# A hybrid decoder step: the sample group's paged attention rebuilt

## The chip, the cores and the metric

One core of a Trainium2 chip runs the whole step. The metric is the device time of one execution in microseconds; the kernel before has a median of 1789.56 us over 3 runs (1787.81 to 1792.38). TensorE (PE) multiplies, VectorE (DVE) and ScalarE (ACT) work element by element, GpSimd (POOL) and SyncE (SP) here mainly issue DMAs.

## The reference, cut to what matters

The step runs one decoder layer for a prompt (256 tokens) and for 8 sample sequences of 4 tokens each (32 tokens), which attend to a paged cache of 2048 past keys. Weights are shared. What the change touches is the sample group's attention:

```python
past_k = cache_k[l][page_table].reshape(8, 2048, 4, 2, 64)   # 16 pages of 128 keys for each sequence
past_v = cache_v[l][page_table].reshape(8, 2048, 4, 128)
# diff_attend, for each sequence b, head h, half c of the head:
s = einsum('bqhcd,bkhcd->bhcqk', q, k) * 64 ** -0.5          # over past and new keys, masked
p = softmax(s)                                               # over all keys
w = p[:, :, 0] - lam * p[:, :, 1]
o = einsum('bhqk,bkhe->bqhe', w, v)                          # then rms_norm over each head's 128
```

All is float32. A page of keys, and one of values, is 128 keys x 512 floats (4 heads x 128), 256 KB; there are 8 x 16 of each. Around it stand: the input projection, a state-space branch, the prompt's attention, gates, branch and output projections, a router, and a mixture of 32 experts (top 4), each with 12 MB of weights.

## The kernel before, in words

Each engine has its own program, and semaphores order them. The stages follow each other: projection (`w_in`), S5 branch and gates, the prompt's attention (to 315 us), sample attention (324 to 607 us), glu, branch, output projections and router (to about 730 us), experts (to 1750 us), and the sum of their rows. Weights and pages go through a ring of 12 slots in SBUF, each 128 partitions x 8 KB (`RING`, L124); a slot is reloaded when TensorE has freed it.

In the experts (33 jobs) each job loads 12 chunks of 1 MB by SP's queue, in a fixed order of slots (`chunk_slot`, L140), and TensorE multiplies them in float32 as two tiles of 64 columns at once, halves of the output.

Sample attention goes by sequences ("batches") i = 0 to 7. A page lies in a quarter of a slot, [128 partitions, 512 floats], loaded by `pages_of` (L421): the page number is read into a register, then one DMA of 128 rows of 2 KB. K0 to K3 (slots 0 to 3) hold the keys, V0 to V3 (4 to 7) the values, four pages each. Keys and the pages of V2 and V3 are issued by SP, V0 and V1 by GpSimd. Each slot is freed when its own pages are used.

For every page TensorE turns the four heads' keys (`keys_turn`, L1039: 4 transposes of 128x128 into one PSUM bank). ScalarE copies the bank, rounded to float32r (`key_high`, L664, recorded as L669), VectorE subtracts this from the bank (`key_low`, L1588, recorded as L1591). The query is split in the same way, high and low beside each other (64 columns), and `scores` (L1051) multiplies it with the high and the low keys, two pages at a time. ScalarE and VectorE add the two halves of the result (`scores_low`, `bank_sum`), VectorE takes the maximum over all keys, ScalarE the exps; these are turned page by page (`exps_turn`), split again, and multiplied with split values (`value_high`, `value_low`, `values`, L1078), all 16 pages into one PSUM bank. The batches are staggered: `batch(i, j)` (L1096) turns and scores batch i while it multiplies the values of batch j = i - 1. Then the sum is divided by the denominator and turned (`out_turn`), the two halves of the head are combined, and after batch 7 all is turned back, normed by head (`head_norm`, L1555) and turned again. The prompt's two tiles are normed just before the first batch.

Transposes are recorded at L893, other matmuls at L890 (a float32 matmul as two records); page DMAs at L428.

Of the kernel before, what the change touches and what calls it, by code (L numbers as in the profile page):

```python
# [32 lines left out]
NB = 8  # L33
# [29 lines left out]
E_STEP = 2  # L63
V_STEP = {3: (0, 3), 4: (3, 7), 5: (7, 10), 6: (10, 13), 7: (13, 16)}
V_BY_SP, V_BY_POOL = (2, 3), (0, 1)
# [5 lines left out]
for _name, _n in [("ident", 128), ("tri", 128), ("iota", CAP), ("ropec", 96), ("ropes", 96), ("tau", W5), ("keep", W5),  # L71
                  ("causal", 256), ("newmask", NB * NSMP), ("ones", 128), ("expert", NE), ("row", 1),
                  ("halves", P), ("jobs", NOVER)]:
    CONST_COLS[_name] = (_at, _n)
    _at += _n
# [3 lines left out]
def constants():  # L79
# [38 lines left out]
    put("halves", (i[:, None] // CAP == i[None, :] // CAP).astype(np.float32))  # L118
    put("jobs", np.broadcast_to(np.arange(NOVER), (P, NOVER)))
# [11 lines left out]
for _name, _s, _d, _r in RING:  # L131
    SLOT[_name], USE0[_name], LOAD0[_name], NDMA[_name] = _s, _uses[_s], _loads[_s], _d
    _uses[_s] += _r
    _loads[_s] += 16 * _d * _r
# [5 lines left out]
def chunk_slot(i):  # L140
    return (i + 1) % NSLOT
# [10 lines left out]
def loaded_at(name, i=0):  # L152

    return LOAD0[name] + 16 * NDMA[name] + i * (16 * NDMA[name])


def free_at(name, i=0):

    return USE0[name] + i
# [4 lines left out]
def numbered(stages):  # L164
    at, out = 0, {}
    for name, n in stages:
# [8 lines left out]
                    ("qk", 6), ("s", 8), ("oS", 1), ("oT", 3), ("bs", 8), ("ba", 8), ("out", 6), ("h2T", 5), ("lg", 3),  # L175
# [3 lines left out]
def build(nc, A):  # L179
    with ExitStack() as ctx:  # L180
# [28 lines left out]
        def at(off, *dims, n=P):  # L209
# [53 lines left out]
        keyh = rounded("keys_high", arena_at + 4 * 2304, [P, 2, H, 2 * P])  # L263
        keyl = rounded("keys_low", arena_at + 4 * (I0 + 3072), [P, 2, H, 2 * P])
        valh = rounded("values_high", arena_at + 4 * I0, [P, 3, 512])
        vall = rounded("values_low", arena_at + 4 * (I0 + 1536), [P, 3, 512])
        e2 = rounded("exps_split", arena_at + 4 * 6912, [P, NPG + 1, 2 * NSMP])
        vnh = rounded("new_values_high", arena_at + 4 * (I0 + 5120), [NSMP, 512])
        vnl = rounded("new_values_low", arena_at + 4 * (I0 + 5632), [NSMP, 512])
        oL = at(4352, 512, n=32)  # L270
        oS = at(4864, 512, n=32)
        ss = ring[0:32, 11, :]
        E = ring[0:32, 10, :]
        sm = I0 + 6144
        snw = at(sm, 32, n=32)
        En = at(sm + 32, 32, n=32)
        mx5 = at(sm + 64, 5, n=32)
        mcol = at(sm + 69, 1, n=32)
        nbias = at(sm + 70, 1, n=32)
        esum = at(sm + 71, 2, n=32)  # L280
        etot = at(sm + 73, 1, n=32)
        rden = at(sm + 74, 1, n=32)
        on = at(sm + 228, H, 2, NS)
        oTs = at(sm + 260, H, NSMP)
# [52 lines left out]
        qs = rounded("queries_split", arena_at + 4 * (K0 + 3104), [P, 72 * H + 32])  # L337
        knh = rounded("new_keys_high", arena_at + 4 * (K0 + 3424), [P, H, NSMP])
        knl = sb("new_keys_low", [P, H, NSMP], mybir.dt.float32r)
# [13 lines left out]
        s_vpool = [sem(f"values_loaded_by_gpsimd{s}") for s in V_BY_POOL]  # L353
# [18 lines left out]
        p_turned, p_keyh, p_keyl, s_group = sem("page_turned"), sem("page_high"), sem("page_low"), sem("group_scored")  # L372
        p_valh, p_vall, p_used = sem("values_page_high"), sem("values_page_low"), sem("values_page_used")
        s_qb, s_newkv, s_new, s_low, s_sum, s_nbias, s_ex, s_rden = (
            sem("q_block"), sem("new_kv_split"), sem("new_scores_done"), sem("scores_low_copied"), sem("scores_summed"),
            sem("max_ready"), sem("sample_exps"), sem("denominators"))
        s_eT, s_eh, s_el, s_pvd, s_oL, s_oS, s_oT, s_do = (
            sem("exps_turned"), sem("exps_high"), sem("exps_low"), sem("sample_pv"), sem("pv_low_copied"), sem("pv_summed"),
            sem("pv_turned"), sem("sample_out"))
# [24 lines left out]
        def wait_loaded(eng, name, i=0):  # L404
            eng.wait_ge(loaded[SLOT[name]], loaded_at(name, i))
# [15 lines left out]
        def pages_of(eng, kind, cache, b, slots=range(4)):  # L421

            for s in slots:
                name = f"{kind}{s}"
                eng.wait_ge(freed[SLOT[name]], free_at(name, b))
                for j in range(4):
                    page = eng.value_load(pages[0:1, ds(b * NPG + (4 * s + j), 1)], min_val=0, max_val=159)
                    eng.dma_start(ring[:, SLOT[name], j * 512:(j + 1) * 512],  # L428
# [96 lines left out]
        def _(act):  # L525
# [165 lines left out]
            def value_high(j, pg):  # L691
                if pg % 4 == 0:
                    wait_values(act, pg // 4, j)
# [1194 lines left out]
```

## Time and profile before

| what | us |
|---|---|
| median of 3 runs | 1789.56 |
| the profiled execution | 1789.9, its span 1788.4 |
| TensorE busy | 1457.9 |
| VectorE busy | 633.5 |
| ScalarE busy | 373.8 |

The page cuts the span into 40 equal slices of 44.7 us; a digit is the busy share in tenths. The chain of waits follows the work that ended last back from the last instruction. A group of the profile names the line, the engine, what is written and read, the shape, the number of instructions, and the mean of one.

### The profile page before, as it was taken

What the parts mean: (1) busy time and instruction counts of PE and PEld (TensorE: products, weight loads), DVE (VectorE), ACT (ScalarE), POOL (GpSimd) and SP (SyncE); (2) the same over time, 40 slices, a digit from 0 to 9 for tenths busy, and PEclk for the clock granted to TensorE, in tenths of its full rate; (3) what the DMA queues carried; (4) which work ended last, traced back from release to release, by engine and by line L of the source; (5) the groups of instructions that cost most, each with busy time, mean ns of one, the idle gap of its engine ahead of it and who ended that gap; (6) DMA issues with size and microseconds to landing.
All of it is one profiled execution on the core that took longest, in us unless ns stands there. A gap on an engine that the chain in (4) does not pass through costs nothing.

```text
span 1788.4 us, 21676 instructions
## 1 busy us (share of the span) xinstructions
PE 1457.9 (82%) x6592; PEld 669.1 (37%) x6592; DVE 633.5 (35%) x1261; ACT 373.8 (21%) x707; POOL 84.4 (5%) x151
## 2 busy tenths in 40 slices
PE   3989656688888798799998988888898989888851
PEld 2537544566666463333222222222222222222210
DVE  1367786688788522711111111111111111111104
ACT  1103223477777401100000000000000000000001
POOL 0000000011001000000000000000000000000003
PEclk7999876799899899799999999999999999999985
DMA  9220024388776822599999999999999999999974
GB/s 386 74 94 1 0 86 150 112 258 252 251 233 199 319 95 113 187 391 419 417 419 417 419 417 420 417 419 418 418 419 417 420 417 419 417 420 417 419 287 138
DMA packets 128849, 536.06 MB, mean 300 GB/s; under 512 B 20721, under 2 KB 21458, under 8 KB 92978
## 3 DMA queue, kind: packets, MB, share of 16 engines
q1 hardware_dynamic: 106914, 493.00, 69.6%
q0 software_dynamic: 10800, 34.87, 5.5%
q10 hardware_dynamic: 11104, 7.80, 1.5%
q8 instruction: 15, 0.25, 0.1%
q14 instruction: 16, 0.13, 0.0%
HBM read 519.75 MB, written 15.88 MB: 300 GB/s over the span
## 4 chain that ended last, share of the span: by engine, by line
PE 29%; DMA 24%; SPq 24%; DVE 13%; issue 6%; ACT 3%; ACTq 1%; POOL 0%; DVEq 0%; POOLq 0%
PE psum L890 24%; DMA ring<-in_w_gate_up 20%; SPq L490 12%; SPq L485 12%; PE psum L893 4%; DMA ring<-in_w_in 2%; DMA ring<-in_w_down 1%; DVE keys_low L1591 1%; DVE values_low L1595 1%; DVE ring L1602 1%; DVE ring L1477 1%; DVE arena L1854 1%; DVE ring L1478 1%; DMA arena<-in_b_down 0%; DMA ring<-expert_rows,rowi 0%
## 5 line engine op out<-in xcount | busy, mean ns | idle before, releaser
L890 PE MATMUL psum<-ring,arena 128*64 128x512 f32 (+3 forms) x3472 | 874.0, 600 | 119.3 <-DMA ring<-in_w_down 69.7
L890 PEld LDWEIGHTS psum<-ring,arena 128*64 128x64 f32 (+2 forms) x3472 | 257.8, 140 | 687.7 <-issue 412.5
L1790 DVE TENSOR_SCALAR arena<-cst,arena 128x64 f32<-128x64 f32 x105 | 20.3, 251 | 435.2 <-PE psum L890 434.9
L890 PE MATMUL psum<-arena 128*64 128x512 f32 (+5 forms) x576 | 143.6, 560 | 36.9 <-ACT ring L608 30.1
L1798 DVE COPY arena<-psum 128x512 f32<-128x512 f32 x34 | 23.5, 692 | 388.9 <-PE psum L890 386.9
L890 PE MATMUL psum<-arena,ring 128*128 128x288 f32 x480 | 129.3, 432 | 14.6 <-DMA ring<-in_w_in 8.9
L893 PE MATMUL psum<-cst,ring 128*128 128x128 f32 (+1 forms) x640 | 93.7, 298 | 35.6 <-DVE keys_low L1591 21.9
L893 PE MATMUL psum<-cst,arena 128*128 128x128 f32 (+2 forms) x455 | 72.7, 285 | 52.6 <-DVE arena L1332 15.5
L890 PEld LDWEIGHTS psum<-arena,ring 128*128 128x128 f32 x480 | 96.4, 203 | 46.1 <-DMA ring<-in_w_in 12.9
L890 PEld LDWEIGHTS psum<-arena 128*64 128x64 f32 (+2 forms) x576 | 65.6, 179 | 106.2 <-issue 61.8
L893 PEld LDWEIGHTS psum<-cst,ring 128*128 128x128 f32 (+1 forms) x640 | 77.8, 158 | 50.6 <-DVE keys_low L1591 28.4
L1591 DVE TENSOR_TENSOR keys_low<-psum,keys_high 128x512 fp32r<-128x512 f32 x128 | 82.2, 679 | 20.3 <-ACT keys_high L669 19.7
L846 POOL DMA_DIRECT2D expert_rows<-arena x66 | 34.4, 522 | 1135.2 <-ACT arena L792 1131.3
L893 PEld LDWEIGHTS psum<-cst,arena 128*128 128x128 f32 (+2 forms) x455 | 52.1, 147 | 93.2 <-issue 70.9
L1595 DVE TENSOR_TENSOR values_low<-ring,values_high 128x512 fp32r<-128x512 f32 x128 | 81.2, 680 | 9.4 <-ACT values_high L696 9.1
L696 ACT ACTIVATE values_high<-ring 128x512 fp32r<-128x512 f32 x128 | 72.4, 619 | 20.4 <-PE psum L890 20.1
L890 PE MATMUL psum<-keys_high,queries_split 128*64 128x256 f32 x256 | 74.8, 321 | 1.1 <-DVE keys_low L1591 1.1
L787 ACT ACTIVATE arena<-arena 128x512 f32<-128x512 f32 x33 | 20.8, 630 | 257.6 <-DVE arena L1802 257.6
L669 ACT ACTIVATE keys_high<-psum 128x512 fp32r<-128x512 f32 x128 | 70.7, 592 | 17.7 <-PE psum L893 16.5
L792 ACT ACTIVATE arena<-psum 128x512 f32<-128x512 f32 x33 | 19.7, 598 | 256.4 <-PE psum L890 256.4
L779 ACT ACTIVATE arena<-psum 128x512 f32<-128x512 f32 x34 | 20.3, 597 | 237.0 <-PE psum L890 237.0
L890 PE MATMUL psum<-keys_low,queries_split 128*64 128x256 f32 x256 | 68.6, 297 | 0.0
(259 smaller groups left out, 1002.6 us busy)
## 6 DMA issues: line engine op xcount, KB each, us to landing
ring<-in_w_gate_up SPq DMA_DIRECT2D x264, 1024.0 KB, 21.2
ring<-in_w_down SPq DMA_DIRECT2D x132, 1024.0 KB, 26.1
ring<-in_cache_k SPq DMA_DIRECT2D x128, 256.0 KB, 3.0
ring<-in_cache_v POOLq DMA_DIRECT2D x64, 256.0 KB, 4.3
ring<-in_cache_v SPq DMA_DIRECT2D x64, 256.0 KB, 3.0
expert_rows<-arena POOLq DMA_DIRECT2D x66, 128.0 KB, 5.8
ring<-in_w_in SPq DMA_DIRECT2D x8, 1024.0 KB, 23.7
ring<-in_w_gate SPq DMA_DIRECT2D x8, 1024.0 KB, 21.3
```

The costliest lines, as they stand in the source:

```text
L485: sp.dma_start(ring[:, s, :], wgu[ds(e, 1), k, :, :].rearrange("o p n -> p (o n)")).then_inc(loaded[s], 16)
L490: sp.dma_start(ring[:, s, :].rearrange("p (k n) -> p k n", k=2), wdn[ds(e, 1), k, :, :, :].rearrange("o p k n -> p (o k) n")).then_inc(loa ...
L669: nc.scalar.activation(keyh[:, g % 2, :, (pg % 2) * P:(pg % 2 + 1) * P], psum[:, pg % 2, :].rearrange("p (h c) -> p h c", h=H), ACT.Copy). ...
L696: nc.scalar.activation(valh[:, pg % 3, :], ring[:, SLOT[f"V{pg // 4}"], (pg % 4) * 512:(pg % 4 + 1) * 512], ACT.Copy).then_inc(p_valh, 1)
L779: nc.scalar.activation(xg, psum[:, 6, :], ACT.Copy).then_inc(e_xg, 1)
L787: nc.scalar.activation(sig, gg, ACT.Sigmoid, scale=ALPHA).then_inc(e_sig, 1)
L846: pool.dma_start(ydram[ds(j * CAP, CAP), 512 * half:512 * half + 512], y[64 * half:64 * half + 64, :]).then_inc(e_out, 16)
L890: return nc.tensor.matmul(out, lhsT=a, rhs=b, start=start, stop=stop, skip_group_check=True)
L893: return nc.tensor.transpose(out, in_, ident[0:n, 0:n])
L1591: TT(keyl[place], psum[:, pg % 2, :].rearrange("p (h c) -> p h c", h=H), keyh[place], ALU.subtract).then_inc(p_keyl, 1)
L1595: TT(vall[:, pg % 3, :], ring[:, SLOT[f"V{pg // 4}"], (pg % 4) * 512:(pg % 4 + 1) * 512], valh[:, pg % 3, :], ALU.subtract).then_inc(p_val ...
L1798: CP(xT[:, :, :], psum[:, 7, :].rearrange("p (c q) -> p c q", c=4)).then_inc(e_xs, 1)
```

## The change

Keys and values are no longer split; everything is multiplied in float32. The 16 pages of a batch are four groups of four. A page goes to 32 partitions, four rows of keys (8 KB) on each, and the four pages of a group fill the 128 partitions of one slot (`four_pages`). Group g's scores are written to partitions 32g to 32g+31 of one bank, each group on a tile of 32 columns of TensorE, and so are its values' products: each group has its own maximum, sum and output. After all batches one merge weighs the groups (`coef`) and turns the heads in the same matmuls. SP issues all keys, GpSimd all values; the values of batch b are loaded when those of b - 1 are multiplied. Branch weights go to slots 0 to 3, `w_out` to 4 to 7 after the last values, and the experts' chunks start at another slot. The sample's head norm is done by a matmul with ones; the prompt's head norms move into the first batches; the glu matmuls stand before the last values.

```diff
-RING += [(f"K{s}", s, 4, NB) for s in range(4)] + [(f"V{s}", 4 + s, 0 if s in V_BY_POOL else 4, NB) for s in range(4)]
-RING += [("w_glu", 8, 1, 1), ("w_bs0", 9, 1, 1), ("w_bs1", 10, 1, 1), ("w_ba0", 11, 1, 1), ("w_ba1", 0, 1, 1)]
-RING += [(f"w_out{k}", 1 + k, 1, 1) for k in range(4)]
+RING += [(f"K{s}", s, 4 * NB, 0) for s in range(4)]
+RING += [("w_glu", 8, 1, 1), ("w_bs0", 0, 1, 1), ("w_bs1", 1, 1, 1), ("w_ba0", 2, 1, 1), ("w_ba1", 3, 1, 1)]
+RING += [(f"w_out{k}", 4 + k, 1, 1) for k in range(4)] + [("exps", 9, 0, 1), ("pv0", 10, 0, 1), ("pv1", 11, 0, 1)]
 def chunk_slot(i):
-    return (i + 1) % NSLOT
+    return (i + 5) % NSLOT
...
+        def four_pages(eng, cache, b, g, s, done):
+            for j in range(4):
+                page = eng.value_load(pages[0:1, b * NPG + 4 * g + j:b * NPG + 4 * g + j + 1], min_val=0, max_val=159)
+                eng.dma_start(ring[32 * j:32 * j + 32, s, :],
+                              cache[ds(page, 1), :, :].rearrange("o (p q) n -> p (o q n)", q=4)).then_inc(done, 16)
...
+            def keys(b, g):                                  # SP
+                if b == 0:
+                    sp.wait_ge(freed[g], USE0[f"K{g}"])
+                else:
+                    sp.wait_ge(s_ktv, 8 * (b - 1) + 2 * g + 2)
+                four_pages(sp, ck, b, g, g, loaded[g])
...
+            sp.wait_ge(s_pvd, NB)                            # before the loads of w_out
...
+            for b in range(NB):                              # GpSimd
+                if b:
+                    pool.wait_ge(s_pvd, b)
+                for g in range(4):
+                    four_pages(pool, cv, b, g, 4 + g, s_vpool[g])
...
+            def turned_keys(i, g):                           # ScalarE: h = 0, 2; VectorE: h = 1, 3
+                for h in (0, 2):
+                    n = 16 * i + 4 * g + h
+                    act.wait_ge(s_turned, n + 1)
+                    if i:
+                        act.wait_ge(s_scored, i)
+                    nc.scalar.activation(KT[g][:, h, :], psum[:, TBANK[n % 4], :], ACT.Copy).then_inc(s_kta, 1)
...
+            def turn_keys(i, g):                             # TensorE from here on
+                pe.wait_ge(loaded[g], keys_at(g, i))
+                for h in range(H):
+                    n = 16 * i + 4 * g + h
+                    if n >= 4:
+                        pe.wait_ge((s_kta, s_ktv)[n % 2], (n - 4) // 2 + 1)
+                    for j in range(4):
+                        last = tr(psum[:, TBANK[n % 4], j * P:(j + 1) * P], ring[:, g, j * 512 + h * P:j * 512 + (h + 1) * P])
+                    last.then_inc(s_turned, 1)
+            def scores(i):
+                pe.wait_ge(s_kta, 8 * i + 8)
+                pe.wait_ge(s_ktv, 8 * i + 8)
...
+                for h in range(H):
+                    for g in range(4):
+                        last = mm(psum[32 * g:32 * g + 32, 3, :], qp[:, h, i, :], KT[g][:, h, :], h == 0, h == H - 1)
+                last.then_inc(s_scored, 1)
...
+            def values(i):
+                pe.wait_ge(s_pT, i + 1)
+                if i:
+                    pe.wait_ge(s_pvs, i)
+                for g in range(4):
+                    pe.wait_ge(s_vpool[g], 64 * (i + 1))
+                mm(psum[0:32, 5, :], pT[0:NSMP, 512:544], vt[0:NSMP, 2, :], True, False)
+                for j in range(4):
+                    for g in range(4):
+                        last = mm(psum[32 * g:32 * g + 32, 5, :], pT[:, j * P + 32 * g:j * P + 32 * g + 32],
+                                  ring[:, 4 + g, j * 512:(j + 1) * 512], j == 0 and g > 0, j == 3)
+                last.then_inc(s_pvd, 1)
...
+            for i in range(NB):
+                turn_keys(i, 0)
+                if i == 0:
+                    new_scores()
+                turn_keys(i, 1)
+                if i:
+                    exps_turn(i - 1)
+                turn_keys(i, 2)
+                turn_keys(i, 3)
+                if i:
+                    values(i - 1)
+                scores(i)
...
+            for i in range(3):
+                glu(i)
+            exps_turn(NB - 1)
...
+            glu(3)
+            values(NB - 1)
...
+            for b in range(NB):
+                for h in range(H):
+                    last = mm(psum[:, 6, h * NSMP + b * NS:h * NSMP + (b + 1) * NS], PV[:, b, h * P:(h + 1) * P],
+                              coef[:, b, h * NS:(h + 1) * NS], True, True)
+            last.then_inc(s_o, 1)
+            pe.wait_ge(s_osq, 1)
+            mm(psum[:, 6, P:2 * P], ones, o_sq, True, True).then_inc(s_osum, 1)
...
+            step(nc.vector.memset(qp, 0.0))                  # VectorE, ahead of the first batch
+            for h in range(H):
+                for c in range(2):
+                    ins = CP(qp[:, h, :, h * QC + c * NS:h * QC + (c + 1) * NS], qsmp[:, h, c])
...
+                if 1 <= i < 3:
+                    head_norm(i - 1, 128)
+                if i < 2:
+                    head_squares(i, 128)
```

## Rows read from the trace of the kernel before

**Rows 1.** The page's 40 slices: DMA share in tenths, GB/s.

```profile
DMA  9220024388776822599999999999999999999974
GB/s 386 74 94 1 0 86 150 112 258 252 251 233 199 319 95 113 187 391 419 417 419 417 419 417 420 417 419 418 418 419 417 420 417 419 417 420 417 419 287 138
```

**Rows 2.** Stretches: length, busy us (count) by engine, PEclk, DMA share, GB/s.

```profile
402.00:436.20 34.20, 28.70 (x192) 22.92 (x193) 28.32 (x56) 24.59 (x45) 4.37 (x8) 0.90 0.78 243
900.00:1300.00 400.00, 352.61 (x1553) 107.71 (x1551) 53.94 (x130) 31.52 (x52) 13.55 (x26) 1.00 1.02 418
```

**Rows 3.** The chain in order of time: start us, us, what.

```profile
419.44 1.97 PE psum L893 x8
453.61 1.97 PE psum L893 x8
```

**Rows 4.** Timeline around the stage: start us, us, engine, line, instruction [idle before <-releaser].

```profile
314.24 0.69 DVE L1550 COPY arena<-psum 128x512 f32<-128x512 f32 x1 [3.43 <-PE psum L890]
324.11 1.94 PE L893 MATMUL psum<-cst,ring 128*128 128x128 f32 x8 [9.91 <-DVEq L1669]
606.53 0.39 PE L890 MATMUL psum<-new_values_low,exps_split 32*64 32x512 f32 x1
610.75 10.44 PE L890 MATMUL psum<-arena,ring 128*128 128x288 f32 x32
624.66 3.78 PE L890 MATMUL psum<-arena,ring 128*128 128x288 f32 x10 [2.24 <-DVE arena L1690]
```

**Rows 5.** Timeline and groups of TensorE: transposes, paired tiles, 32-column matmuls, their weight loads.

```profile
405.70 1.03 PE L893 MATMUL psum<-cst,ring 128*128 128x128 f32 x8
1003.82 1.94 PE L890 MATMUL psum<-ring,arena 128*64 128x512 f32 x8 [0.54 <-DMA ring<-in_w_gate_up]
...
L890 PE MATMUL psum<-ring,arena 128*32 128x512 f32 x80 | 34.7, 593 | 0.1
L890 PEld LDWEIGHTS psum<-ring,arena 128*32 128x32 f32 x80 | 8.6, 110 | 25.3 <-issue 25.0 <-DVE arena L1357 0.3
```

**Rows 6.** Issue of pages, then of expert rows, then DMA issues (KB, us to landing).

```profile
402.62 0.55 POOL L428 DMA_DIRECT2D ring<-in_cache_v  x1 [0.67 <-issue]
403.84 0.55 POOL L428 DMA_DIRECT2D ring<-in_cache_v  x1 [0.67 <-issue]
412.55 8.47 SPq L428 DMA_DIRECT2D ring<-in_cache_v  x8
...
L846 POOL DMA_DIRECT2D expert_rows<-arena x66 | 34.4, 522 | 1135.2 <-ACT arena L792 1131.3
...
ring<-in_cache_v POOLq DMA_DIRECT2D x64, 256.0 KB, 4.3
ring<-in_cache_v SPq DMA_DIRECT2D x64, 256.0 KB, 3.0
```

**Rows 7.** Timeline: value matmuls behind idle, and warm ones.

```profile
594.06 0.69 PE L890 MATMUL psum<-values_high,exps_split 128*64 128x512 f32 x1 [1.56 <-DVE exps_split L1624]
598.45 0.54 PE L890 MATMUL psum<-values_high,exps_split 128*64 128x512 f32 x1
...
404.32 0.40 PE L890 MATMUL psum<-values_high,exps_split 128*64 128x512 f32 x1
404.55 0.39 PE L890 MATMUL psum<-values_low,exps_split 128*64 128x512 f32 x1
```

**Rows 8.** Stretches with narrow transfers (first two) and a wide one (last).

```profile
718.00:720.00 2.00, 2.00 (x12) 2.00 (x11) 1.13 (x6) 0.00 (x0) 0.00 (x0) 0.50 1.03 218
1751.00:1752.00 1.00, 0.00 (x0) 0.00 (x0) 0.00 (x0) 0.00 (x0) 0.00 (x0) 1.00 0.69 160
1784.00:1786.00 2.00, 0.00 (x0) 0.00 (x0) 1.67 (x3) 0.00 (x0) 0.00 (x0) 0.50 0.83 336
```

**Rows 9.** A memset, and the group of the router's matmuls.

```profile
276.61 1.98 DVE L1510 MEMSET arena<- 128x2304 f32 x1 [0.76 <-PE psum L893]
L890 PE MATMUL psum<-arena 128*128 128x32 f32 x32 | 7.0, 401 | 0.6 <-issue 0.6
```

More of the change, by code:

```diff
@@ L62 @@
 NSLOT = 12
[L63 to L65 removed]
+TBANK = (0, 1, 2, 6)
 N_SMALL = 15
@@ L352, in build @@
         s_vec = sem("vectors_in")
-        s_vpool = [sem(f"values_loaded_by_gpsimd{s}") for s in V_BY_POOL]
+        s_vpool = [sem(f"values_loaded{s}") for s in range(4)]
         s_const, s_x, s_par, s_pages = sem("consts_in"), sem("x_in"), sem("params_in"), sem("pages_in")
@@ L419, in build @@
         xin = [xp[0:128, :], xp[128:256, :], xs]
[L421 to L428, printed above, removed]
-                                  cache[ds(page, 1), :, :].rearrange("o p n -> p (o n)")).then_inc(
-                                      s_vpool[s] if eng is nc.gpsimd else loaded[SLOT[name]], 16)
-        def wait_values(eng, s, j):
-            if s in V_BY_POOL:
-                eng.wait_ge(s_vpool[s], j * 64 + 64)
-            else:
-                wait_loaded(eng, f"V{s}", j)
+        def four_pages(eng, cache, b, g, s, done):
[3 more added lines that the diff above has]
+                              cache[ds(page, 1), :, :].rearrange("o (p q) n -> p (o q n)", q=4)).then_inc(done, 16)
         @block.sync
@@ L442, in load @@
             def load(name, src, dst=None):
-                if free_at(name):
+                if free_at(name) and not name.startswith("w_out"):
                     sp.wait_ge(freed[SLOT[name]], free_at(name))
@@ new lines, in exps @@
+            def exps(i):
+                act.wait_ge(s_nbias, i + 1)
+                if i:
+                    act.wait_ge(s_eT, i)
+                nc.scalar.activation(E[0:32, 512:544], snw[:, i * NSMP:(i + 1) * NSMP], ACT.Exp, scale=SCALE,
+                                     bias=nbias[0:32, i:i + 1], accum_out=esum_new[:, i:i + 1])
+                nc.scalar.activation(E[:, 0:512], psum[:, 3, :], ACT.Exp, scale=SCALE, bias=nbias[:, i:i + 1],
+                                     accum_out=esum[:, i:i + 1]).then_inc(s_ex, 1)
@@ L1118, in _ @@
             pe.wait_ge(s_pvr, 2)
             pe.wait_ge(act_done, ACT_JOB["glu"])
-            pe.wait_ge(dve_done, DVE_JOB["oS"])
-            pe.wait_ge(s_newkv, 1)
-            batch(0, None)
-            with pe.Fori(1, NB) as i:
-                batch(i, pe.snap(i - 1))
-            pe.wait_ge(s_ex, NB)
-            pe.wait_ge(s_do, NB - 1)
-            exps_turn()
-            for pg in range(NPG):
-                values(NB - 1, pg)
-            new_values()
-            pe.wait_ge(s_oS, NB)
@@ L1144, in _, with glu @@
+            def glu(i):
                 b = abank()
@@ L1147, in _ @@
                 last.then_inc(act_full, 1)
-            for t, (t0, n) in enumerate(TILES):
+            assert na[0] % 4 == 0
+            wait_loaded(pe, "w_glu")
+            pe.wait_ge(s_gelu, 1)
+            for i in range(3):
+                glu(i)
+            exps_turn(NB - 1)
+            pe.wait_ge(s_stat, 1)
+            tr(psum[0:NB, 6, 2 * P:3 * P], smax)
+            tr(psum[0:NB, 6, 3 * P:4 * P], esum).then_inc(s_statT, 1)
+            glu(3)
+            values(NB - 1)
+            pe.wait_ge(s_cT, 1)
+            tr(psum[:, 7, 3 * P:3 * P + NB], tdif, NB).then_inc(s_coef, 1)
+            pe.wait_ge(s_pvs, NB)
+            pe.wait_ge(s_cf, 1)
+            for b in range(NB):
+                for h in range(H):
[4 more added lines that the diff above has]
+            mm(psum[:, 6, P:2 * P], ones, o_sq, True, True).then_inc(s_osum, 1)
+            pe.wait_ge(s_do, 1)
+            for name in ("exps", "pv0", "pv1"):
+                pe.sem_inc(freed[SLOT[name]], 1)
+            for t, (t0, n) in enumerate(TILES[0:2]):
                 pe.wait_ge(s_ln, t + 1)
```

470 lines of the change are left out of this document (155 added, 315 removed).

## The prediction

> **What bounds the kernel now.** Read the 40 slices of the page first [rows 1]. From the 18th slice on (about 760 us) the DMA row stays at 9 and the rate at 417 to 420 GB/s: the experts stream 1 MB weight chunks, and the stretch 900 to 1300 us shows 418 GB/s at a DMA share of 1.02 [rows 2]. Nothing in the diff touches that stream, so whatever comes before it moves the end one for one. Sample attention is the stretch with 250 GB/s. In the chain of waits the same piece (eight key transposes) returns at 419.44 and 453.61 us, and so on [rows 3]: a batch takes 34.17 us and there are eight. In one such batch TensorE is busy 28.7 of 34.2 us, VectorE 28.3, ScalarE 24.6, and DMA has a share of 0.78 at 243 GB/s [rows 2]. So TensorE's order of work, with short waits for the two splitting engines, bounds a batch; DMA is not far behind (8.39 MB at 243/0.78 = 312 GB/s would take 26.9 us). The stage runs from the first turn at 324.1 to the last value matmul at 606.53 + 0.39 = 606.9, and the next stage's matmuls start at 624.66 [rows 4].
>
> **Part 1, TensorE's work.** Before, key pages are turned (64 transposes), multiplied in two parts (64 + 8 records), exps turned (17), values multiplied in two parts (34). Warm, 8 transposes take 1.03 us [rows 5], and they stay: 64 x 0.129 = 8.3 us. A float32 matmul appears as two records. In the experts, two 64-column tiles run at once: 8 records of 512 columns in 1.94 us, a pair of records each 0.43 us [rows 5]. A single 32-column matmul costs the same 0.43 (34.7 us busy / 80) with a weight load of 0.11 us [rows 5]. If four 32-column tiles overlap as two do, 16 score matmuls are 32 records = 8 x 0.43 = 3.4 us, the values 3.4 + 0.9 for the new keys = 4.3 us, exps turned 5 x 0.129 = 0.65. Four weight loads of 0.11 = 0.44 just fit under 0.43. Bounds: 0.43 for four (taken, nearest the paired row), 0.86 (only pairs), 1.7 (none). TensorE's sum is 16.7 us a batch where it had 28.7.
>
> The Trainium skill, TensorE: Matmul & The Clock Gate, Part 3, gives a measured 2.38 times for three column tiles. By that rate a group of four would cost about 0.54 us and the whole some 8 us more (an estimate from that page); the trace has no four tiles to compare.
>
> **Part 2, the copies.** 32 splits of keys and values on ScalarE and 32 subtractions on VectorE go. Left are 16 copies of a bank of 128x512, eight on each engine. VectorE takes 0.69 us for one [rows 4], so 5.5, and for maximum, exps and values out, four more passes of this size, 2.8; ScalarE has its eight and two exps, 6 to 7. Neither bounds a batch of 17 us. Costed at nothing, hidden by TensorE; with TensorE at 16.7 they still have 8 us in hand.
>
> **Part 3, who loads what, and when.** Before, 8 of 16 value pages come by GpSimd's queue, 8 by SP's, and a slot is refilled as soon as its four pages are used. After, all 16 value pages are issued by GpSimd, and only when the values of the batch before are finished (wait for `s_pvd`). So a closed loop appears: value pages issued, landed, multiplied, then the next issue. Its terms:
> - GpSimd issues a page every 1.22 us (402.62, 403.84) [rows 6], so 16 take 19.5 us. No row shows 32 rows of 8 KB; 64-row issues take 0.52 us where 128-row ones take 0.55 [rows 6], so shorter lists gain a few hundredths. I keep 1.22.
> - Landing: 4.3 us median from issue for GpSimd's, 3.0 for SP's [rows 6]; less about 1 of moving, 3.3 us.
> - Values: 4.3 us warm. TensorE has then stood idle for long. After the idle at the end of the loop of before, the granted clock fell: value matmuls come every 0.43 us for 4.4 us (594.06 to 598.45), where warm ones come every 0.23 [rows 7]. 4.4 us at half rate do 2.2 us of the work, 2.1 are left: 6.5 us.
> With free DMA the loop is 19.5 + 3.3 + 6.5 = 29.3 us. It replaces TensorE as the bound; SP's keys (1.06 us a page, 8.47 for 8 [rows 6], 17 us a batch) lie beside it.
>
> **Part 4, the new layout in SBUF.** This decides. A page now goes to 32 partitions, 8 KB on each. Which rows show narrow transfers? At 718 to 720 us only the bias loads are left in flight (32 partitions each, 2 and 4 KB rows): the DMA engines are fully busy (1.03) and move 218 GB/s, half of the expert stream's 418 at 1.02 [rows 8, 2]. Near the end the last expert rows go out from 64 partitions: 160 GB/s at 0.69, that is 232; a write from 128 partitions shows 336 at 0.83, that is 405 [rows 8]. In both narrow cases transfers to the lower and the upper half were queued one behind the other and it did not help. So a page costs 262144 B / 218 GB/s = 1.20 us of all the engines, where a page in 2 KB rows over 128 partitions costs 0.84 (at 312). A batch of 32 pages needs 38.4 us instead of 26.9. Bounds: 1.24 us (218/1.03 = 212 GB/s, the same row at a share of 1) and 0.63 (418); taken 1.20, from the row of the same direction, loads.
>
> The Trainium skill, SBUF — State Buffer, Door 1, explains it: partitions 0 to 31, or 0 to 63, reach 8 of 16 DMA ports, about 218 GB/s at best, the figure of the row. It adds that two transfers to the two halves gain 6% together. By that, 231 GB/s, the sum below would end near 1803 (an estimate); no row here has two narrow queues at once.
>
> **The loop with this.** After values are done: scores 3.4, one group turned 2.1, its copy 1.0: 6.5 us in which value pages are alone, 5.3 issued at 1.22. Then key pages (SP's queue) share the engines; I take equal shares, so the other 10.7 value pages take 2 x 1.20 = 2.40 each, 25.7 us. Loop: 6.5 + 25.7 + 3.3 + 6.5 = 42.0 us. Keys left over (5.3 pages, 6.4 us) move while the last values land and are multiplied. Value pages of batches 1 to 5 meet keys: 5 x 42.0 = 210. Those of batch 6 meet the four branch weights instead (4 MB wide, 0.63 per 256 KB): 6.5 + 10.7 x 1.83 + 9.8 = 35.9. Batch 7's are alone: 29.3. The first loop also meets 6 key pages of batch 2: +3. Sum 278 us.
>
> **Start.** The prompt's last copy ends at 314.9, the first turn comes at 324.1 [rows 4]: two head norms and the splits between them leave the front; a memset of 1024 columns (1.98 x 1024/2304 = 0.9 us [rows 9]) and eight small copies (0.2 each) come. Transposes start at 315.0, cold: 16 take 3.9 us (8 in 1.97 [rows 3]); new scores, 64 records at 0.06, 3.7 and a wait of 1.3; three groups, partly cold, 7; scores 4.2; batch 1 turned, exps 9; values 4.3 plus 1 of slack. Values of batch 0 are done at 349. The stage ends at 349 + 278 = 627, where it ended at 606.9: +20.3 us.
>
> **Tail.** Before, 17.8 us lie between the last value matmul and 624.66: sums, turns, the glu matmuls (10.44 us [rows 4]), three head turns, a product. After, the glu moves into the loop's idle time. New in its place: out copy and waits 1.5; 32 merge matmuls with 128-column weights, 64 records. A row of like shape has 32 records in 7.0 us at the low clock [rows 9]; warm I take 0.14, 9 us (bounds 7 and 14). Then square, ones matmul, table load, root, scale 3.7; turns, copies, product 3.6. Sum 17.8: no change. `w_out` (4 MB) is now loaded after the loop; 40 us of branch matmuls cover its 10. One expert chunk more waits until `w_out`'s slots are free, on the queue beside the biases at 714 us: +1.
>
> Total 1789.9 + 20.3 + 1 = **1811 us**; the profiled execution's 1789.9 lies 0.3 above the median of the runs.
>
> **Rivals.**
> *A, the halves mix.* With keys and values on two queues, a key page for one half may move beside a value page for the other. If half the pages do, the rate is 2/(1/218 + 1/418) = 287 GB/s, a page 0.91 us. Loops: 6.5 + 10.7 x 1.83 + 9.8 = 35.8, then 32.8 and 29.3; sum 243, end of stage 592: 1776 us, faster. For it: two queues, issue rates that differ. Against: engines fully busy at 218 with both halves queued [rows 8].
> *B, the width costs nothing* and 8 KB rows move as in the experts (418). Then only GpSimd's issue counts: 7 x 29.3 = 205, end at 554, 1738 us. For it: the descriptors are four times longer. Against: rows 8.
> *C, four tiles run only as pairs.* Values 9.9 us behind idle instead of 6.5, scores 6.9 instead of 3.4. The longer scores hold back the keys, which gives the value pages a longer start, so the shared loops hardly change (42.1); the front (+10) and the last loops (+7) do: 1828 us. For it: four weight loads just fit. With A it would cost more of the gain.
> The change of sign lies at about 255 GB/s for narrow pages: above it the loop falls under about 39 us and the stage ends before 607.
>
> **How the numbers follow.** The forecast 0.53 (its own range, 212 to 245 GB/s and 5 us either way at front and tail: 1790 to 1821), A 0.21, B 0.14, C 0.12. A measurement of this kernel tells 0.3%, 5.4 us, from no change. Faster: B, most of A, 0.01 of C: 0.34. Within: edges of A and of the forecast, 0.05. Slower 0.61. The range 1762 to 1840 leaves out B and the far ends.
>
> **What would show it.** A period between value stages of about 42 us with DMA share near 1 and 200 to 235 GB/s in the middle batches, TensorE waiting for the value pages (`s_vpool`) before each value stage; values at the low clock first; batch 7's loop under 31 us; page landing times grown well above 4.3 us. Wrong: a period under 36 us, a DMA rate above 280 GB/s there, value matmuls not overlapping by four, or a tail off from 18 us by more than 5.

## The result, and the profile after

The kernel after takes **1845.66 us** (median of 4 runs, 1841.46 to 1847.27) where the kernel before takes 1790.97 in the same runs (4, 1787.81 to 1793.09): a ratio of 1.0303 [1.0279, 1.0328]. It is slower, as forecast, but by 54.7 us and not by 21; the time lies above the forecast's range of 1762 to 1840. The profiled execution has a span of 1843.4 us, 55.0 more than before's.

The first view is again the 40 slices, now of 46.1 us. The rows that answer to [rows 1]:

```profile
DMA  9220055988888742479999999999999999999974
GB/s 388 58 92 1 0 140 136 221 181 198 183 187 200 202 160 91 142 269 419 418 418 418 418 418 418 419 418 418 418 419 417 419 418 418 418 418 418 418 288 134
```

The expert stream is the same (418). In sample attention (slices 8 to 13) the DMA digits are 9 and 8 where before's slices 9 to 13 had 8 to 6, and the rate is 181 to 221 GB/s where it was 199 to 258: busier engines move less.

Next the stretches. First comes what answers to [rows 2, 8]; the three rows after the dots are the waits between two value stages, of the first loop, an ordinary one and the last; the final two are two value stages. The columns are those of [rows 2].

```profile
403.00:407.00 4.00, 3.01 (x29) 2.73 (x26) 3.66 (x8) 2.63 (x7) 1.84 (x4) 1.00 0.87 211
407.00:411.00 4.00, 4.00 (x37) 3.79 (x36) 3.38 (x6) 1.89 (x4) 1.58 (x4) 1.00 1.03 219
415.00:419.00 4.00, 0.00 (x0) 0.00 (x0) 0.00 (x0) 0.00 (x0) 1.56 (x4) 0.62 1.02 229
...
344.90:391.50 46.60, 13.86 (x102) 10.05 (x95) 10.56 (x19) 6.97 (x14) 7.83 (x16) 0.68 1.02 219
442.20:480.60 38.40, 11.22 (x101) 8.22 (x94) 7.92 (x14) 5.50 (x12) 7.83 (x16) 0.69 0.93 202
619.00:646.60 27.60, 12.29 (x72) 7.34 (x65) 4.57 (x14) 7.24 (x12) 7.84 (x16) 0.78 0.77 195
...
391.50:399.70 8.20, 8.20 (x38) 1.75 (x42) 0.00 (x0) 0.00 (x0) 0.00 (x0) 0.55 0.30 66
435.40:442.20 6.80, 6.79 (x38) 1.50 (x42) 0.00 (x0) 0.00 (x0) 0.00 (x0) 0.67 0.64 139
```

The reader is to see full engines (1.02, 1.03) at 219 to 229 GB/s, the rate of the bias loads [rows 8], now over long stretches and with both halves of the partitions in flight. TensorE is busy 11.2 of 38.4 us there. The best stretches show 229, 5% over 219; no view says which halves were in flight in them.

The waits say who is late (engine, line <- releaser: us in all, times, longest), and the page's DMA issues how long a page takes (KB, us from issue to landing):

```profile
PE psum L838 <- DMA ring<-in_cache_v: 165.8, 7, 27.2
...
ring<-in_cache_k SPq DMA_DIRECT2D x128, 256.0 KB, 11.3
ring<-in_cache_v POOLq DMA_DIRECT2D x128, 256.0 KB, 8.5
```

TensorE waits for values before seven of the eight value stages, 23.7 us each time on the mean, 165.8 in all. Landings on SP's queue went from 3.0 us [rows 6] to 11.3, on GpSimd's from 4.3 to 8.5.

The value stages in the chain of waits (start us, us, what):

```profile
340.31 4.58 PE psum L838 x34
391.48 8.26 PE psum L838 x34
435.41 6.78 PE psum L838 x34
480.60 8.07 PE psum L838 x34
526.66 7.23 PE psum L838 x34
571.57 6.96 PE psum L838 x34
611.53 7.46 PE psum L838 x34
646.58 7.00 PE psum L838 x34
```

From start to start the seven loops take 51.2, 43.9, 45.2, 46.1, 44.9, 40.0 and 35.1 us, where a batch took 34.17 [rows 3]. The timeline around one of them and at the stage's end (columns as [rows 4]):

```profile
435.41 1.88 PE L838 MATMUL psum<-arena,ring 32*32 32x512 f32 x2 [23.24 <-DMA ring<-in_cache_v]
437.22 4.91 PE L838 MATMUL psum<-ring 128*32 128x512 f32 x32
441.96 3.61 PE L838 MATMUL psum<-arena 128*32 128x512 f32 x32
...
654.64 10.46 PE L838 MATMUL psum<-arena,ring 128*128 128x4 f32 x64 [0.95 <-DVE arena L1577]
665.43 1.28 ACT L696 ACT_TABLE_LOAD   x1
673.31 2.26 PE L838 MATMUL psum<-arena,ring 128*128 128x288 f32 x4 [2.25 <-DVE arena L1588]
774.80 1.48 ACT L713 ACTIVATE bias_split<-arena 128x1536 fp32r<-128x1536 f32 x1 [19.66 <-DMA arena<-in_b_down]
```

At the high clock, the 32 records of the 32-column score matmuls take 3.61 us, 0.45 for each four, where one record alone takes 0.43 [rows 5]: four column tiles do run together. The merge takes 10.46 us. The branch matmuls start at 673.31, 48.65 us later than before (624.66, [rows 4]).

### The profile page after: what moved, and what is told of

Its sections match the earlier page's. It is cut to its first block, busy times and chain, and to the rows that moved or that the text cites. A ratio compares the mean times of both kernels' runs of the same rounds, so it can differ in the third digit from the quotient of the medians.

```text
span 1843.4 us, 19302 instructions
## 1 busy us (share of the span) xinstructions
PE 1389.2 (75%) x6269; PEld 580.7 (32%) x6269; DVE 469.2 (25%) x944; ACT 226.5 (12%) x450; POOL 111.9 (6%) x214
## 4 chain that ended last, share of the span: by engine, by line
DMA 31%; SPq 24%; PE 22%; DVE 10%; issue 8%; POOLq 2%; POOL 1%; ACT 1%; ACTq 0%; DVEq 0%
PE psum L838 21%; DMA ring<-in_w_gate_up 20%; SPq L474 11%; SPq L469 11%; DMA ring<-in_cache_v 7%; POOLq L420 2%; DMA ring<-in_w_in 2%; DMA ring<-in_w_down 1%; POOL ring L421 1%; PE psum L841 1%; DMA arena<-in_b_down 1%; DVE ring L1412 1%; DVE arena L1752 1%; DVE ring L1413 1%; POOLq L421 0%
## 5 line engine op out<-in xcount | busy, mean ns | idle before, releaser
L838 PE MATMUL psum<-arena,ring 128*128 128x288 f32 (+2 forms) x560 | 152.6, 430 | 180.8 <-DMA ring<-in_cache_v 165.8
L838 PE MATMUL psum<-arena 128*64 128x512 f32 (+6 forms) x896 | 175.2, 545 | 36.9 <-ACT ring L592 29.2
L838 PEld LDWEIGHTS psum<-arena,ring 128*128 128x128 f32 (+1 forms) x560 | 107.4, 206 | 214.6 <-issue 171.2
L1696 DVE COPY arena<-psum 128x512 f32<-128x512 f32 x34 | 23.5, 691 | 389.6 <-PE psum L838 387.6
L838 PEld LDWEIGHTS psum<-arena 128*64 128x64 f32 (+2 forms) x896 | 75.9, 156 | 125.6 <-issue 81.3
L421 POOL DMA_DIRECT2D ring<-in_cache_v x128 | 62.7, 490 | 572.1 <-issue 572.1
L841 PE MATMUL psum<-cst,ring 128*128 128x128 f32 (+1 forms) x552 | 68.7, 283 | 13.8 <-DMA ring<-in_cache_k 6.2
L841 PEld LDWEIGHTS psum<-cst,ring 128*128 128x128 f32 (+1 forms) x552 | 63.0, 145 | 23.3 <-issue 12.1
L655 ACT ACTIVATE arena<-psum 128x512 f32<-128x512 f32 x64 | 37.1, 591 | 216.0 <-PE psum L841 216.0
L737 ACT ACTIVATE arena<-psum 128x512 f32<-128x512 f32 x33 | 19.7, 598 | 258.0 <-PE psum L838 258.0
L724 ACT ACTIVATE arena<-psum 128x512 f32<-128x512 f32 x34 | 20.3, 598 | 237.3 <-PE psum L838 237.3
L1511 DVE COPY arena<-psum 128x512 f32<-128x512 f32 x64 | 44.0, 691 | 19.1 <-PE psum L841 17.9
L728 ACT ACTIVATE arena<-psum 128x512 f32<-128x512 f32 x33 | 19.7, 598 | 189.7 <-PE psum L841 189.7
L838 PE MATMUL psum<-ring 128*32 128x512 f32 x256 | 42.3, 822 | 0.0
## 6 DMA issues: line engine op xcount, KB each, us to landing
ring<-in_cache_k SPq DMA_DIRECT2D x128, 256.0 KB, 11.3
```

What stands on the lines that cost most here:

```text
L421: eng.dma_start(ring[32 * j:32 * j + 32, s, :], cache[ds(page, 1), :, :].rearrange("o (p q) n -> p (o q n)", q=4)).then_inc(done, 16)
L655: nc.scalar.activation(KT[g][:, h, :], psum[:, TBANK[n % 4], :], ACT.Copy).then_inc(s_kta, 1)
L724: nc.scalar.activation(xg, psum[:, 6, :], ACT.Copy).then_inc(e_xg, 1)
L838: return nc.tensor.matmul(out, lhsT=a, rhs=b, start=start, stop=stop, skip_group_check=True)
L841: return nc.tensor.transpose(out, in_, ident[0:n, 0:n])
L1511: CP(KT[g][:, h, :], psum[:, TBANK[n % 4], :]).then_inc(s_ktv, 1)
```

## The experiments

Two theories stood against each other at first. **W**: the layout costs the time, because a page in adjacent partitions moves at half the rate. **R**: something else about 8 KB rows, or about GpSimd alone issuing the values, costs it, and the width does not. The expectations also carry **I**: GpSimd's issue and the single set of value slots set the loop, whatever the rate. Times are medians. The kernel before was measured on the same chip each time (medians 1788.8 to 1791.2), and differences between kernels of different chips are taken from the ratios, times 1790.

### The page as wide as before

```diff
-                eng.dma_start(ring[32 * j:32 * j + 32, s, :],
-                              cache[ds(page, 1), :, :].rearrange("o (p q) n -> p (o q n)", q=4))
+                eng.dma_start(ring[:, s, j * 512:(j + 1) * 512],
+                              cache[ds(page, 1), :, :].rearrange("o p n -> p (o n)"))
```

> Only the layout of a page is undone: 128 partitions with 2 KB on each, as before; queues, waits and matmuls as in the changed kernel. Theory W (few partitions give the DMA engines half their rate): the middle batches run at 290 to 320 GB/s instead of 220 to 229 with the engines full, a page costs 0.84 us instead of 1.17, the loop from values to values falls from 45 to about 36 us, 1795 us. Rival I (GpSimd's issue and the single set of value slots set the loop, the rate is not what counts): loop and time stay, 1846 us. Rival R (not the partitions but the 8 KB rows, two to an engine, are slow): the same as W here, so the next kernels are needed.

1765.27 us, ratio 0.9859 [0.9832, 0.9885]. Nothing but the shape of 256 page transfers differs from the kernel after, and 80 us are gone (1.0303 less 0.9859), 30 more than expected. Loops are 32.5 us on the mean, not 36, and the landing of keys is 5.1 us where it was 11.3. Theory I, by which nothing would change, falls as it stands; what is left of it comes back below.

### The same rows, spread over all partitions

Each page keeps its 32 rows of 8 KB, but on every fourth partition: j, j + 4, ... and no longer 32j to 32j + 31.

```diff
-                eng.dma_start(ring[32 * j:32 * j + 32, s, :],
+                eng.dma_start(ring[j:P:4, s, :],
```

> Rows stay 8 KB and 32 to a page, issues and descriptors as in the changed kernel; page j goes to the partitions j, j+4, j+8 ... 124 instead of 32j to 32j+31. Theory W: the rate rises towards the experts' 418 GB/s, the loop is then GpSimd's issue (18 us), 4 us of start and landing and 7 us of values, 30 us; 1755 us. Where engines that share a place keep in step, something between 1755 and 1846. Rival R (8 KB rows): nothing changes, 1846 us. Rival I: 1846 us.

1761.91 us, ratio 0.9856 [0.9817, 0.9895], the same as with 2 KB rows. The stretch 440 to 560 us, first of the kernel after, then of this one:

```profile
440.00:560.00 120.00, 51.19 (x391) 28.61 (x383) 23.76 (x42) 16.50 (x36) 23.50 (x48) 0.71 0.84 184
```

```profile
440.00:560.00 120.00, 75.16 (x510) 38.31 (x508) 28.30 (x56) 23.72 (x48) 32.72 (x61) 0.78 0.69 241
```

Share 0.84 for 184 GB/s became 0.69 for 241: at a share of one, 219 against 349 GB/s. Row length and number of partitions are equal in both, so it is neither the 8 KB rows nor 32 rows as such: **adjacent** partitions are slow. (349 is an estimate from a share below one.) R falls. No step other than four was run. The Trainium skill, SBUF — State Buffer, Door 1, gives the port of a partition by bits 2 to 4 and 6 of its number; a step of four then reaches all 16 ports, 32 adjacent ones only eight. The runs agree.

### 64 adjacent partitions, rows of 4 KB

```diff
-                eng.dma_start(ring[32 * j:32 * j + 32, s, :],
-                              cache[ds(page, 1), :, :].rearrange("o (p q) n -> p (o q n)", q=4))
+                eng.dma_start(ring[64 * (j // 2):64 * (j // 2) + 64, s, (j % 2) * 1024:(j % 2 + 1) * 1024],
+                              cache[ds(page, 1), :, :].rearrange("o (p q) n -> p (o q n)", q=2))
```

> A page on 64 adjacent partitions with 4 KB on each. Theory W in the form of the Trainium skill, SBUF - State Buffer, Door 1 (partitions 0 to 63 reach no more ports than 0 to 31): the rate stays near 225 GB/s, 1846 us within 8. Rival R (row length or number of rows to an engine): between e1_wide2k and the changed kernel, about 1820 us.

1833.72 us (1828.6 to 1849.7, the widest spread of any kernel here, and the trace is of the longest), ratio 1.0235 [1.0204, 1.0267]. Twice the partitions bring back 12 of the 80 us, 4 more than theory W allowed, and keys land in 10.1 us. Its rate varies between full stretches:

```profile
415.00:419.00 4.00, 3.00 (x26) 2.55 (x25) 3.61 (x8) 2.20 (x7) 1.64 (x4) 1.00 1.02 231
418.00:442.00 24.00, 4.14 (x37) 3.90 (x36) 4.21 (x7) 2.52 (x5) 4.84 (x10) 0.66 1.03 250
```

Over 440 to 560 us it is 194 GB/s at 0.85, 228 at a full share against the changed kernel's 219. So the count of partitions matters little, and which they are matters much.

### Keys and values at opposite halves

The prediction's rival A: GpSimd takes each group's pages in the order 2, 3, 0, 1, so that its page tends to lie in the other half than SP's.

```diff
-            for j in range(4):
+            for j in ((2, 3, 0, 1) if eng is nc.gpsimd else range(4)):
```

> The changed kernel with the value pages of a group issued in the order 2, 3, 0, 1, so that value pages for the upper half of the partitions go out beside key pages for the lower half. Theory W with engines in step: no change, 1846 us within 5. Rival A of the prediction (the halves mix and the rate is up to 287 GB/s): the middle loops fall by 4 to 9 us, 1800 to 1820 us.

1839.16 us, ratio 1.0267 [1.0239, 1.0296], 6.5 us below the kernel after, and its interval reaches into that one's. The four middle loops take 43.5 us on the mean where they took 45.0. The rate, however, did rise. The same stretch, first of the kernel after, then of this one, with only narrow pages of both queues in flight:

```profile
466.00:482.00 16.00, 1.40 (x2) 0.18 (x2) 0.00 (x0) 0.00 (x0) 0.00 (x0) 0.50 1.03 216
```

```profile
466.00:482.00 16.00, 1.36 (x2) 0.18 (x2) 0.00 (x0) 0.00 (x0) 0.00 (x0) 0.50 1.03 258
```

258 GB/s with full engines is a fifth above 216, so in this one trace rival A's mixing exists in part. It doesn't last: 418 to 442 us of the same run show 213 at 1.02, and 440 to 560 us 193 at 0.81, 238 at a full share. Which page stood beside which in flight isn't ordered by this edit, so it is not shown what a strict alternation of the halves would bring; 287 was reached over none of these stretches. The Trainium skill, SBUF — State Buffer, "Can I just issue two DMAs to hit both halves?", puts the gain of two transfers to the two halves at 6%. Here the measurement decides: 19% over 16 us, 9% over 120.

### Narrow pages, issue divided

Is the closed loop of GpSimd a cost by itself? Value groups 2 and 3 are issued by SP, behind the keys of the next batch.

```diff
+            def values_half(b):
+                sp.wait_ge(s_pvd, b)
+                for g in (2, 3):
+                    four_pages(sp, cv, b, g, 4 + g, s_vpool[g])
...
-                for g in range(4):
+                for g in range(2):
                     four_pages(pool, cv, b, g, 4 + g, s_vpool[g])
```

> The changed kernel with its narrow pages (32 adjacent partitions), but the value pages of groups 2 and 3 issued by SP, as the kernel before had it: each queue issues half. Theory W: 32 narrow pages still cost 37 us of full DMA engines and values cannot start before; loops fall from 45 to 41 to 44 us only, 1815 to 1840 us. Rival I (GpSimd's issue of 16 pages, 18 us, is in the loop): loops fall by 8 to 9 us each, 1785 us.

1811.17 us, ratio 1.0116 [1.0099, 1.0132]. That is 4 us better than theory W had it and far from the 1785 of theory I. Loops are 37.3 to 38.0 us up to the last, of 30.9:

```profile
350.00:500.00 150.00, 84.15 (x566) 48.30 (x563) 38.45 (x68) 26.98 (x55) 15.67 (x32) 0.75 1.02 225
```

The engines are full for 150 us on end; 32 pages at 225 GB/s are 37.3 us, which is the loop. So of the changed kernel's 43.9 to 46.1 us some 37.5 are bytes at the narrow rate, and 6 to 9 are time in which the closed loop leaves the engines partly idle, around the values. Opening it is worth 34 of the 54.7 us.

### Spread and divided

> Pages spread over every fourth partition and the value pages of groups 2 and 3 issued by SP. With the rate restored the loop was 32.3 us, of it 18 us GpSimd's issue; halved, values can start about 14 us after the last ones ended; then SP's own issue (24 pages at 1.03 us, 24.7 us) is the bound: loops of 25 to 26 us, 1762 - 7 x 6.5 = 1716 us. If the DMA rate were again the bound, loops above 30 us and no gain.

```diff
-                eng.dma_start(ring[32 * j:32 * j + 32, s, :],
+                eng.dma_start(ring[j:P:4, s, :],
...
+                for g in (2, 3):
+                    four_pages(sp, cv, b, g, 4 + g, s_vpool[g])
```

1750.29 us, ratio 0.9763 [0.9745, 0.9782], 34 us above the expectation. The timeline of SP's queue names the next bound:

```profile
406.69 20.17 SPq L421 DMA_DIRECT2D ring<-in_cache_k  x16
427.63 9.07 SPq L421 DMA_DIRECT2D ring<-in_cache_v  x8
437.46 19.32 SPq L421 DMA_DIRECT2D ring<-in_cache_k  x16
457.56 9.07 SPq L421 DMA_DIRECT2D ring<-in_cache_v  x8
```

SP issues without a pause, 24 pages in 29.9 us (427.63 to 457.56), 1.25 each, and not at 1.03 as the expectation had it. Loops are 30 us: once the rate is restored, issue is the bound. The same queue is slower with the spread pages: the eight value pages that take 9.07 us here took 7.79 in the narrow kernel with the same division:

```profile
438.51 7.79 SPq L421 DMA_DIRECT2D ring<-in_cache_v  x8
```

### The values loaded once

> Spread pages; the value pages are loaded for the first batch only, later batches multiply the same ones (the output is then not the reference's). It shows what is left of a batch without the value loop: TensorE's 16.7 us or SP's 16 key pages at 1.03 us, so 17 to 19 us, values matmuls warm at 4.6 us and four column tiles at 0.44 us a group. 1762 - 7 x 14 = 1664 us. If the tiles or the copies were the hidden bound, batches of 25 us and more.

```diff
-            for b in range(NB):
-                if b:
-                    pool.wait_ge(s_pvd, b)
+            for b in range(1):
...
-                    pe.wait_ge(s_vpool[g], 64 * (i + 1))
+                    pe.wait_ge(s_vpool[g], 64)
```

1648.61 us (2 runs), ratio 0.9206 [0.9187, 0.9224]. The output is another, and with it the routing: 384 chunks of 1 MB of expert weights are loaded where all others load 396. One job of 12 MB less is about 30 us at 418 GB/s (an estimate), so some 30 of the 113 us below the spread kernel are not the loop's.

The value stages start 20.0 us apart on the mean (345.98 to 465.91, six loops). That is not TensorE's own pace but SP's issue of keys. The queue's timeline, TensorE's waits from 385 to 487 us, and the stretch of two batches:

```profile
395.35 64.30 SPq L421 DMA_DIRECT2D ring<-in_cache_k  x52
...
PE psum L839 <- DMA ring<-in_cache_k: 10.2, 5, 3.1
...
385.08:425.99 40.91, 34.15 (x272) 20.66 (x272) 15.86 (x28) 11.20 (x25) 0.00 (x0) 0.94 0.74 210
```

52 pages in 64.3 us are 1.25 each, 20 for sixteen. TensorE is busy 17.1 us a batch at a mean clock of 0.94; the prediction's 16.7, all at the high clock, hold. Without the value loop SP's issue is the next bound.

### The biases earlier

> e6_spread_split with the eight bias loads issued when the branch results are merged instead of after the router's turns. In the changed kernel the biases landed 11.0 us after their last issue (8.3 before) and ended the wait ahead of the first expert. If that wait is on the path: 3 to 6 us below e6_spread_split. If the first expert's chunks come no earlier either: no change.

```diff
+            act.wait_ge(s_mg, 1)
+            for half in range(2):
...
+                    act.dma_start(braw[rows_, 0:D], A["b_gate_up"][0][:, D * half:D * half + D]).then_inc(s_bias, 16)
+                    act.dma_start(braw[rows_, D:1536], A["b_down"][0][:, 512 * half:512 * half + 512]).then_inc(s_bias, 16)
```

This stands on top of the spread and divided kernel. The eight loads, which stood further down on ScalarE, now follow the merge weights. 1745.23 us, ratio 0.9746 [0.9729, 0.9764]: 5 us by the medians, 3 by the ratios, and as the two intervals overlap the gain is not shown.

### Twelve value pages by GpSimd, four by SP

On top of the last kernel, where it was eight and eight.

```diff
-                for g in (2, 3):
+                for g in (3,):
                     four_pages(sp, cv, b, g, 4 + g, s_vpool[g])
...
-                for g in range(2):
+                for g in range(3):
                     four_pages(pool, cv, b, g, 4 + g, s_vpool[g])
```

> e8_final with twelve value pages of a batch issued by GpSimd and four by SP, where it was eight and eight. In e6_spread_split SP issued its 24 pages in 29 us (16 keys in 19 to 20, 8 values in 9) and the loop was 30 us: if SP's issue is the bound, it falls to 24 us and GpSimd's twelve (1.2 + 13.7 us), landing 4 and values 7.4 make the loop 27 us: 1745 - 7 x 3 = 1724 us. If something else holds the loop at 30 us (value landing, the clock), no change.

1739.69 us, ratio 0.9723 [0.9706, 0.9741]: little better, with overlapping intervals, and 16 us above what was expected. Its loops follow each other at 28.1 us; in the chain of waits:

```profile
375.42 6.32 PE psum L851 x34
403.56 6.77 PE psum L851 x34
431.59 8.10 PE psum L851 x34
459.74 7.68 PE psum L851 x34
```

In the first of these loops the last of GpSimd's twelve pages is issued 14.0 us after the values' end (381.74), lands 7.8 later, and 6.3 of values had gone before: 28.1. The landing was expected at 4. The bound has moved from SP's issue to GpSimd's pages.

### Eight by GpSimd, eight by ScalarE

```diff
+                if i > 1:
+                    act.wait_ge(s_pvd, i - 1)
+                    four_pages(act, cv, i - 1, 2, 6, s_vpool[2])
                 turned_keys(i, 0)
                 if i:
                     exps(i - 1)
+                if i > 1:
+                    four_pages(act, cv, i - 1, 3, 7, s_vpool[3], (0, 1))
                 turned_keys(i, 1)
+                if i > 1:
+                    four_pages(act, cv, i - 1, 3, 7, s_vpool[3], (2, 3))
...
+            act.wait_ge(s_pvd, NB - 1)
+            four_pages(act, cv, NB - 1, 2, 6, s_vpool[2])
             exps(NB - 1)
+            four_pages(act, cv, NB - 1, 3, 7, s_vpool[3])
```

This is the kernel with the early biases again; SP issues keys alone, but for batch 0's groups 2 and 3.

> Rows of each page on every fourth partition, bias loads early (as in the kernel of 1745 us), and of a batch's 16 value pages 8 issued by GpSimd and 8 by ScalarE between its copies, SP issuing keys alone. Theory that issue bounds the loop: GpSimd's 8 pages take 9.1 us, SP's 16 keys 16 to 20 us, so that the values wait for 9 + 6 to 7 us of landing and the loop falls to 22 to 25 us (from 28.0 in the 12-and-4 division and 30 in the 8-and-8 one by SP): 1700 to 1715 us. Rival: ScalarE's eight issues at 1.1 us (9 us a batch) hold back the copies of turned keys and the exponentials, the loop goes to 27 to 30 us: 1730 to 1750 us.

**1722.6 us** (1721.1 to 1729.7), ratio 0.9636 [0.9607, 0.9666], the fastest kernel here with the reference's output. The loops fell as the issue theory said, and the time is 8 us above its range.

```profile
457.92 6.28 PE psum L852 x34
483.08 7.70 PE psum L852 x34
508.25 7.07 PE psum L852 x34
531.05 7.61 PE psum L852 x34
```

```profile
350.00:500.00 150.00, 113.68 (x802) 61.07 (x800) 50.13 (x90) 34.31 (x73) 25.22 (x47) 0.85 0.91 321
```

Six loops from 382.20 to 531.05 take 24.8 us on the mean (22.8 to 26.1), the engines move 321 GB/s at 0.91, and 32 pages at 321/0.91 = 353 would take 23.8 (an estimate). So the loop now stands close to the transfer itself. In the chain of waits the last page of a loop lands 6.1 to 9.4 us after its issue, where 6 to 7 were said; in two of five loops that page is ScalarE's, in three GpSimd's.

## Why the prediction was right in sign and wrong in size

**The step that decides** (part 4) held: narrow pages move at 219 to 229 GB/s with full engines, forecast 218, and the layout alone turns a change that is 27 us faster (spread, 1761.91 against 1788.78) into one that is 55 slower. Rival B is refuted by the same runs. The point of sign at 255 GB/s is only bracketed: slower at 219 to 238 at a full share, faster at 349.

**The failed step is "The loop with this"**: 42.0 us a shared loop, 278 for all. The mechanism (issue, landing, values in a closed loop over slow pages) was right; the terms of the first and last rounds and of the values were too small. Measured from the end of values(0) at 344.9 to 653.6 they are 308.7, 31 more; the earlier start (344.9, forecast 349) gives 4 back, so the stage ends at 653.6 and not 627. Loop by loop, the wait from the end of values to the next values against the forecast's:
- The first loop: 46.6 against 38.5. The forecast counted 6 more key pages and put them at +3. The trace has the engines at 1.02 for all 46.6 us and 219 GB/s: 39 pages, 16 of values and some 23 of keys, which SP issues as the turns free their slots. At full engines a further page costs its whole 1.20 us, and 6 cost 7 and not 3. The rest is some 3 pages more: 35.5 us at 1.20 are 29.6 pages, 16 of values and 13.6 of keys, and 6 more make 19.6 keys and not 23.
- The four shared ones after it: 35.7, 38.4, 37.7 and 38.0 against 35.5, +7.8 in all. GpSimd starts 1.2 us behind the values (399.74, 400.92), its issue is 1.14 us and not 1.22, but the last page, issued at 418.02 in the second loop, lands only at 435.3, behind keys.
- The last two: 33.0 and 27.6 against 29.4 and 22.8, +8.4. In the last one the value pages were taken as alone and bound by their issue. But 16 narrow pages want 19.2 us of all engines and their issue 18.2, and the 27.6 us at 195 GB/s are 5.4 MB, the pages' 4.2 and a reload of x by ScalarE's queue beside them.
- The values themselves: seven behind idle take 6.8 to 8.3 us, mean 7.4, against 6.5: +6.3. If the clock has its two levels alone, a mean of 0.67 over 6.8 us is 4.5 us at the low one, as forecast (4.4), but 0.55 over 8.2 is 7.4.

Together +30.6 of the 30.7. That the parts add up follows from how they are cut; the causes given are read from one trace, and no run changed the edges alone. What was neglected is of one kind: pages and time were counted for the steady loop alone, and its shares (equal between two queues) were taken for the edges too. In the steady loop 42.0 stands against 45.0, the mean of the four.

**TensorE's four tiles** (part 1): held. 3.61 us for scores where 3.4 was said; rival C is refuted. The Trainium skill, TensorE: Matmul & The Clock Gate, Part 3, has 2.38 times for three column tiles. Here four records, one of each tile, take 0.45 us where one takes 0.43 (34.7/80) [rows 5], nearly four times, and not the 0.54 worked out from that page.

**TensorE's sum** (part 1), 16.7 us a batch, is borne out by the 17.1 of the kernel that loads the values once.

**The copies** (part 2): cost nothing, as said; VectorE is busy 7.9 and ScalarE 5.5 us a loop.

**Tail**: 19.7 us (653.6 to 673.31) against 17.8; the merge is 10.46 against 9, between its bounds.

**Behind it**, +1 was forecast and +6.4 measured (48.65 at the branches, 55.0 at the end): 0.9 up to the last bias issue (714.00, 763.58), 2.9 more of waiting for the biases (they land 11.2 us after that issue, before 8.3), and 2.5 spread over the experts and the sum of their rows. Why the biases land later was not found. Issuing them early took 3 to 5 us off, which is in accord but within the noise.

26.4 of the stage, 1.9 of the tail and 5.4 behind it are the 33.7 us by which the span missed.

Rival A got a chance of 0.21 on a mixing of halves. In the kernel after, with both halves in use, the rate was 219 to 229 GB/s, so the forecast's choice held for it. Its reason, that halves queued together did not help [rows 8], does not hold in general: the opposite order reached 258 over 16 us.

The seven loops of the spread kernel take 224.4 us (342.53 to 566.91), those of the changed one 306.3, 11.7 a loop less. The prediction's two prices for a page, 1.20 and 0.84 us, put 11.5 between 32 pages, but that agreement is luck: the spread loops are not full of transfer (share 0.69), and the prediction's own formula at 0.84 gives 6.5 + 10.7 x 1.68 + 9.8 = 34.3, 7.7 less than 42.0.

Still open: how two queues' pages share the engines (no view gives it by page), why the low clock lasts 4.5 us in one value stage and 7.4 in another, and why SP issues eight value pages in 9.07 us when they are spread, 7.79 when adjacent and 8.47 in the kernel before [rows 6].

## What to carry to other kernels

Before a transfer is laid over a group of adjacent partitions, look in the trace for any narrow one and read its rate at a full share; if it is half, keep the rows and spread them with a step (here `j:128:4`), which costs one index and gave 80 us. When one slot set is both loaded and used once a batch, write the loop down as issue + landing + use and count what the other queues have in flight at its first and last rounds, not only in the middle. Then divide the issue over every queue that is idle, and count each queue's whole load: with the values all on GpSimd the loops took 32 us, with 8 of them put behind SP's 16 keys 30 (SP the bound), with 12 on GpSimd and 4 on SP 28, and with 8 on GpSimd and 8 on ScalarE 25. And when a test run computes something else, check that what follows still does the same work.

## What the runs showed of the hardware

- 32 rows of 8 KB: 219 GB/s at a full share on adjacent partitions (184/0.84), 349 (241/0.69, an estimate) on every fourth. 64 adjacent partitions with 4 KB rows: 228 (194/0.85).
- Two queues with narrow pages in both halves: 216 to 229 GB/s in the kernel after; with the values' order turned round 238 at a full share over 120 us, and 258 over the best 16. The two halves do mix, but not dependably.
- Page issue with a page number read from memory: 1.14 us on GpSimd; on SP 7.79 us for eight adjacent pages and 9.07 for eight spread ones, 1.25 each over 52 spread keys. ScalarE gave eight a batch between its copies; in two of five loops its page was the last to land.
- Four 32-column float32 tiles: 32 records in 3.61 us at the high clock.
